# Products that nobody reads, put on TensorE ahead of its waits in a two-block transformer kernel

## What is computed

```python
def hier_moe(h, w_rg, b_rg, w_re, b_re, w_gate, w_up, w_down):
    ...
    pg = jax.nn.softmax((t @ w_rg).astype(jnp.float32) + b_rg.astype(jnp.float32), axis=-1)
    ptop, gsel = lax.top_k(pg, 1)
    ...
    lv, li = lax.top_k(le_g, MOE_TOPK)
    ...
```

```python
    for l in range(DEPTH_2):
        ...
        n = _modulate(_rms_norm(h, norm_g[l, 0]), sh1, sc1)
        h = h + 0.5 * ga1 * _swiglu(n, ffn_w_in[l, 0], ffn_w_out[l, 0])
        n = _modulate(_rms_norm(h, norm_g[l, 1]), sh2, sc2)
        h = h + ga2 * _token_mixing(n, mix_w_in[l], nsa_cmp_pe[l], nsa_cmp_w1[l], nsa_cmp_w2[l],
        ...
        n = _modulate(_rms_norm(h, norm_g[l, 2]), sh3, sc3)
        h = h + 0.5 * ga3 * _swiglu(n, ffn_w_in[l, 1], ffn_w_out[l, 1])
    return _rms_norm(h, final_norm_g)
```

## Time and profile before

| What | Value |
|---|---|
| median of three executions | 2030.01 us |
| lowest and highest of them | 2023.62, 2030.46 us |
| span of the profiled execution | 2027.0 us |
| TensorE busy | 1927.8 us (95%) |
| VectorE busy | 1377.5 us (68%) |
| ScalarE busy | 987.9 us (49%) |
| GpSimd busy | 85.2 us (4%) |
| mean granted clock of TensorE | 0.976 |
| moved by DMA | 458.42 MB, mean 226 GB/s |

### The profile page before, as it was taken

One profiled execution on the slowest core, in us unless ns is written; L12 is line 12 of the kernel. 1 busy time (PEld: TensorE's weight loads), 2 busy tenths in 40 slices (PEclk: granted clock), 3 DMA queues, 4 the chain that ended last, 5 costly groups with the idle time before them and its releaser, 6 DMA issues.

```text
span 2027.0 us, 29852 instructions
## 1 busy us (share of the span) xinstructions
PE 1927.8 (95%) x12628; PEld 1716.6 (85%) x12656; DVE 1377.5 (68%) x1463; ACT 987.9 (49%) x1147; POOL 85.2 (4%) x107
## 2 busy tenths in 40 slices
PE   7989989999997999999998999999999999989998
PEld 3977778888886999899877899989998997769997
DVE  4889668899896877766345787777766452465444
ACT  3356457777775434454444433353335444445342
POOL 1330100000001000000000000000001000000000
PEclk9989989999998999999998999999999999899999
DMA  8555449998994787565212587659774541134554
GB/s 364 210 212 220 174 167 348 351 375 342 351 371 185 281 301 269 221 237 185 86 71 96 203 331 294 246 194 334 290 267 150 184 185 65 63 114 179 186 187 156
DMA packets 63877, 458.42 MB, mean 226 GB/s; under 512 B 7040, under 2 KB 7296, under 8 KB 8832
## 3 DMA queue, kind: packets, MB, share of 16 engines
q1 hardware_dynamic: 63744, 456.51, 59.6%
HBM read 455.43 MB, written 1.05 MB: 225 GB/s over the span
## 4 chain that ended last, share of the span: by engine, by line
PE 58%; issue 24%; DVE 11%; ACT 4%; DVEq 1%; DMA 1%; POOL 1%; POOLq 0%; SPq 0%; ACTq 0%
PE PS L359 16%; PE PS L361 16%; PE PS L360 16%; DVE acc L332 4%; DVE wlo L286 3%; ACT whi L280 2%; PE PS L345 1%; PE PS L1257 1%; PE PS L967 1%; PE PS L1329 1%; PE PS L1341 1%; PE PS L2082 1%; POOL Z L491 0%; DMA raw<-in_stream 0%; PE PS L939 0%
## 5 line engine op out<-in xcount | busy, mean ns | idle before, releaser
L286 DVE TENSOR_TENSOR wlo<-raw,whi 128x2048 fp32r<-128x2048 f32 x282 | 646.9, 2296 | 334.4 <-ACT whi L280 329.2
L280 ACT ACTIVATE whi<-raw 128x2048 fp32r<-128x2048 f32 x282 | 538.6, 1913 | 351.8 <-PE PS L361 308.5
L359 PE MATMUL PS<-whi,hhi 128*128 128x256 f32 (+1 forms) x1568 | 505.4, 322 | 25.7 <-DVE wlo L286 13.3
L360 PE MATMUL PS<-wlo,hhi 128*128 128x256 f32 (+1 forms) x1568 | 493.5, 315 | 0.0
L361 PE MATMUL PS<-whi,hlo 128*128 128x256 f32 (+1 forms) x1568 | 493.1, 314 | 0.0
L359 PEld LDWEIGHTS PS<-whi,hhi 128*128 128x128 f32 x1568 | 304.1, 194 | 50.6 <-issue 22.4
L359 PE MATMUL PS<-hhi,whi 128*128 128x256 f32 x1152 | 326.9, 284 | 2.9 <-DVE mod L354 2.9
L361 PE MATMUL PS<-hhi,wlo 128*128 128x256 f32 x1152 | 326.0, 283 | 0.0
L360 PE MATMUL PS<-hlo,whi 128*128 128x256 f32 x1152 | 325.9, 283 | 0.0
L361 PEld LDWEIGHTS PS<-whi,hlo 128*128 128x128 f32 x1568 | 303.7, 194 | 17.4
L360 PEld LDWEIGHTS PS<-wlo,hhi 128*128 128x128 f32 x1568 | 304.2, 194 | 15.6
(11 more groups left out here) (398 smaller groups left out, 1777.4 us busy)
## 6 DMA issues: line engine op xcount, KB each, us to landing
raw<-in_stream SPq DMA_DIRECT2D x285, 1024.0 KB, 4.9
ada<-in_ada SPq DMA_DIRECT2D x92, 1024.0 KB, 4.9
ada<-in_stream SPq DMA_DIRECT2D x48, 1024.0 KB, 4.9
raw<-in_ada SPq DMA_DIRECT2D x3, 1024.0 KB, 15.5
xs<-in_x SPq DMA_DIRECT2D x1, 1024.0 KB, 11.5
Z<-in_ada SPq DMA_DIRECT2D x1, 1024.0 KB, 19.4
Z<-in_ctx SPq DMA_DIRECT2D x1, 1024.0 KB, 10.7
masks<-in_masks SPq DMA_DIRECT2D x2, 512.0 KB, 9.6
```

The costliest lines, as they stand in the source:

```text
L280: nc.scalar.activation(whi[:, s], src, ACT.Copy).then_inc(hi_ready, 1)
L286: nc.vector.tensor_tensor(wlo[:, s], src, whi[:, s].bitcast(F32), ALU.subtract).then_inc(lo_ready, 1)
L359: nc.tensor.matmul(out_, ah, bh, start=start, stop=False, skip_group_check=check)
L360: nc.tensor.matmul(out_, ah, bl, start=False, stop=False, skip_group_check=check)
```

## The change

The change adds products whose result no instruction reads. A helper, `keep_busy(n, bank)`, multiplies the zeros in `zb` (128x128 by 128x512, bf16) n times into a PSUM bank that is free there. In the opening, where `zb` isn't used, three float32 products of constants with 512 columns stand instead. Nothing is removed, and nothing is moved. Other engines' lists are the same. Two waits are added on TensorE, each so that the bank is free before zeros are written to it: for `m_out` at 10 ahead of the 8, and for `br_out` at 1 ahead of the 7.

| Place | Added | Ahead of the wait for |
|---|---|---|
| opening | 3 float32 products, 512 columns | `hlo` (L1626) |
| router, after `norm_pe` | 9 | `hlo` (L468) |
| router, before the count | 6 | DVE's choice of groups (L1171) |
| before the gather | 5 | positions (L1205) |
| after the gather | 8 | `hlo` of the gathered tile |
| experts' end | 30 | `xn` (L412) |
| before the first feed-forward network | 9 | `hlo` (L468) |
| each layer, pass loop's last two steps | 8 and 6 | exponential (L2242) |
| each layer, merged result's turns | 7 and 15 | DVE Z (L2555), and `wlo` (L286) |

```diff
+        def keep_busy(n, bank):
+
+            for _ in range(n):
+                nc.tensor.matmul(PS[:, bank], zb[:, 0:P], zb[:, :], start=True, stop=True)
...
             for t in range(NT):
                 nc.tensor.matmul(PS[:, 2, 72:76], ones, a0[:, 4 * t:4 * t + 4], start=t == 0, stop=t == 1)
+            keep_busy(5, 5)
             moe_gather_pe(pe, 0)
+            keep_busy(8, 5)
             pe.wait_ge(*N1.row.at(1))
...
                     if half:
                         ins.then_inc(y_sum, 1)
+            keep_busy(30, 3)
...
             cols(3).then_inc(*ada_cols.up)
+            for _ in range(3):
+                nc.tensor.matmul(PS[:, 5], ident, k1[:, 0:512], start=True, stop=True)
...
             norm_pe(pe, N1, 2, 0, 1, xn, TB)
+            keep_busy(9, 7)
             router(1).then_inc(*logits.up)
+            keep_busy(6, 7)
             moe_pe(pe)
...
                 norm_pe(pe, N2, 0, 0, 0, xn, TB)
                 pe.wait_ge(*N1.x_new.at(3))
+                keep_busy(9, 7)
...
+                if i == PASSES2 - 1:
+                    pe.wait_ge(*B["m_out"].at(10, l))
+                    keep_busy(8, 7)
+                if i == PASSES2:
+                    keep_busy(6, 7)
                 if 1 <= i <= PASSES2:
...
+            pe.wait_ge(*B["br_out"].at(1, l))
+            keep_busy(7, 5)
             turn_merged(0)
             turn_merged(1)
...
             turn_merged(3)
+            keep_busy(15, 1)
             pe.wait_ge(*B["y2_lo"].at(4, l))
```

## The result

The changed kernel took 2017.97 us (median of four executions, 2013.85 to 2018.98), the kernel before 2029.43 us beside it (four executions). The ratio is 0.9941, 95% interval [0.9929, 0.9953]: faster by 11.5 us, where 14.8 were forecast. Run again later it took 2014.61 us (five executions, 2013.24 to 2014.95), ratio 0.9925 [0.9912, 0.9939], or 15.0 us. The ratios leave out two executions that lay far off, 2140.35 us of the kernel before and 6622.29 us of the kernel with the experts' end alone. The profiled execution is the slowest of the first four, 2018.98 us.

A forecast was written before the change was run, and what follows sets the result against it. TensorE was taken to bound the kernel, with products after its waits running at half clock. Gains by place, 0 + 3.7 + 1.5 + 6.2 + 3.4 = 14.8 us, off 2030.0 gave 2015.2 us; range 2009 to 2025.

The forecast's parts named there:

- Zeros hold the clock: At all fills: dense 512-column products of zeros count as work and keep TensorE's clock full; no row showed it directly.
- fills that don't hold: Rival, chance 0.07: zeros don't count, the clock still falls and fills overrun their waits; 9.0 us slower, 2039.0 us.
- Experts' end: From the experts' last transposes to the second half's: transposes and 48 head products at full clock win 1.5 us, bounds 0.5 to 2.6.
- The new last one: Before the second half's transposes: GpSimd's and ACT's chain, not the clock, limits the gain to 1.5 us.
- Passes' end: Last passes and gate's projection at full clock: 2.3 plus 0.8 us won, 3.1 a layer, 6.2 in all.
- nine products after the merged result: Output products after the merged turns: 2.1 us at full clock against 3.72, winning 1.7 us a layer, 3.4 in all.
- Router and gather: From the router to the first expert products: 1.9, 2.6 and 0.9 us to win, 5.4 together, taken as 3.7.
- the step that discounted: At router and gather: sparse products may still drop the clock, fills overrun by about 1 us; two thirds of 5.4 taken.
- Opening: First slow stretch, 38.91 to 45.74 us: any gain is waited away for DVE's `wlo`; 0 us, bounds -0.3 and +0.3.
- nothing to be seen: Rival, chance 0.13: falls come elsewhere between executions and gains get lost one by one; 2026 to 2030 us.
- The next late engine: Rival, chance 0.23: loads in the experts stage or DVE's `wlo` take back 7.1 us, leaving 7.7; 2022.3 us.
- Half of all slow time: Rival, chance 0.04: of 65.0 us slow time in the stretches with fills, 32.5 come back; 1997.5 us.

The follow-up runs named there:

- the kernel with the experts' end alone: Only the 30 zero products before the second half's transposes and the 9 behind them added to the kernel before: 2029.27 us, ratio 0.9992.

## Why the prediction was right

The forecast of 2015.2 us lies 2.8 us below the first median and 0.6 above the second, and both are inside its range. The mechanism held place by place; that the total came so close is partly luck. In the first pair of traces 9.8 us were won, 5.0 short of the sum of 14.8, and the medians (11.5) were kinder than that pair. The fills won slightly more than the sum, and falls that it had no term for took some of that back. The second median is near because layer 1 was spared a fall of 3.05 us that no fill stands ahead of.

**Zeros hold the clock.** Right: four stretches went from 0.50 to 1.00, and 60 zeros held it for 13 us. The price of 0.23 us was right too: 30 took 6.65 us. The rival of fills that don't hold (2039.0) is out; the short fill of 20-column products shows what it would have looked like, without the overruns. It came true at one place, told below.

**Experts' end**, 1.5 forecast: 1.45 three times. The new last one is the one named, ACT's `xn`, with a wait of 0.82 us where about 1 was expected.

**Passes' end**, 3.1 a layer: 2.76 and 2.66. The mechanism held and the term was 0.4 too large: of the 2.3 us forecast for the work from 1066.95 to 1071.55, 2.1 came, and of the 0.8 for the gate's projection 0.7. The nine products after the merged result took 2.12 us (1101.77 to 1103.89), as said, and won 1.61 and 1.64 where 1.7 were forecast.

**Router and gather**, 3.7: here the step that discounted was half right. The fills won 4.9 and 5.7 us, where the upper bound was 5.4; the gather took 3.84 us. In the first trace a fall came in spite of the fills, as said, during `router(1)`, the six zeros behind it ran at half clock (2.74 us for a wait of 1.50 before), and TensorE was through with them 0.95 us after the choice of groups that they were to cover. The discount had foreseen just this, an overrun of about 1 us; a fill that ends after what it waits for was also named as a sign of being wrong. From the last router product's result on DVE to the 0/1 matrix of the gather this trace took 4.44 us (253.17 to 257.61), the second, in which the six took 1.47 us, 3.62 (252.89 to 256.51): 0.8 us lost, about the difference between 4.9 and 5.7. The trace with 60 zeros at the experts' end shows the same overrun. The fall near 279 then took 1.6 back, which no step had. Net 3.35 and 4.04. Of the eleven traces this fall is in five of the six with the router's fills of 512 columns, and missing only where zeros stand among the sparse products. It is in none of the five without, four of which are slow as late as 271 to 273 us instead. The fall was moved, not only removed.

**Opening**, 0: -0.60 and -0.26. The first lies outside its bounds of 0.3, and traces without any fill there scatter by 2.2 us at the same landmark. The term of 0 isn't contradicted, and isn't shown to some tenths either: the clock there was full in one trace, which won nothing.

**What the sum lacked** is the row that no part of it had: other falls. Each term was sized as if the rest of the program kept its clock history. At the compressed branch and in the second feed-forward network of layer 0 the changed kernel lost 1.5 to 1.6 us each, and in layer 1's compressed branch it lost nothing or won 3.05. Of the rivals "nothing to be seen" named the scatter, but as a case of its own and not as a term beside the gains. The range had 3 us of scatter upwards, less than the 4.6 us that falls took in the first trace; what kept the time well inside is that the range also took in a rival.

**The next late engine** didn't take anything back. TensorE was busy for 340.00 of 340.00 us between 280 and 620 us, as before:

```profile
280.00:620.00 340.00, 340.00 (x1598) 283.51 (x1597) 299.24 (x187) 253.10 (x188) 0.00 (x0) 1.00 0.90 348
```

and the wait for `wlo` in the first expert grew by 0.54 us (1.01 against 0.47 before), where the prediction allowed it half of 1.7.

**Half of all slow time** would have been 32.5 us in the treated stretches; 15.0 to 15.8 came back. The rule of the Trainium skill (TensorE: Matmul & The Clock Gate, section Terms) prices slow time by its length; the trace doesn't agree. By the windows of the eight stretches at half clock that make up the prediction's 65.0 us (there are two at each layer's end and three at the router), TensorE was busy for 50.5 of 64.9 us, and the other 14.3, half of them at the experts' end, are waits, which didn't shrink. Another 6.8 us at half clock near the router are still there in each trace of the changed kernel. And what products won at the experts' end was in part waited away for ACT (0.82 us). How the missing 17 us divide among these isn't shown.

## What to carry to other kernels

Price a fall of the clock by the products that run in it and by who waits for them, not by its length; then fill the wait ahead with dense products and leave room at its end (0.1 to 1.0 us were left here), since each zero too many costs its full 0.22 us, and twice that where the clock has already fallen. The places of 7.5 and 3.9 us of waiting fell in every trace without a fill there, and so did the passes' end, with waits of 2.0 and 1.5 us close together; a single wait of 2.2 us fell in 3 of 10. So look at more than one trace for what falls each time, fill that, and expect the other falls to add or take 1.5 to 3 us at places that weren't touched. Judge such a change by the start of the same instruction in both traces, because a gain of 1.5 us is plain there and can't be seen in the total time.

## What the runs showed of the hardware

Products of zeros keep the clock up: in the kernel with 60 of them the engine multiplied nothing but zeros for 13.12 us at full clock. And a fall can come in the midst of alternating products of 512 and of 64 columns: it came at 971.5 us, and the last pause of the engine that the trace shows, 0.24 us, ended at 968.7.
